# Order of projections, openings and turns, and products of constants in TensorE's waits, in a transformer forward pass of three mixers

## The reference

```python
def conv_ffn(h, w_up, conv_w, conv_b, w_down):
    u = causal_conv3_per_channel(h @ w_up) + conv_b
    gate, val = jnp.split(u, 2, axis=-1)
    return (jax.nn.silu(gate) * val) @ w_down      # 1024 -> 2 x 2816 -> 1024

# mixer 1: 12 heads of 64, causal softmax attention with a learned decay, q and k normed by head
# mixer 2: latent queries (256) and keys/values (128), 12 heads of 96 (64 plain, 32 rotary), causal
# mixer 3: 8 query heads and 2 key heads of 64, window of 128, partial rotary, a sink logit per head,
#          beside a gated depthwise convolution of 31 taps with layer norm and silu
# each mixer also attends to a memory of 256 tokens (4 heads of 64), and all parts go through w_out
```

## Time and profile before

| what | value |
|---|---|
| median of 3 runs | 2228.28 us (2227.41 to 2228.83) |
| profiled execution | 2224.88 us |
| its span | 2223.1 us, 30649 instructions |
| TensorE products busy | 2117.9 us (95%), 11378 |
| TensorE weight loads busy | 1759.9 us (79%) |
| VectorE busy | 1274.8 us (57%), 2212 |
| ScalarE busy | 952.9 us (43%), 1912 |
| GpSimd busy | 33.7 us (2%) |
| mean granted TensorE clock | 0.982 |
| HBM | 187.36 MB moved, 84 GB/s |

### The profile page before, as it was taken

How to read it: one execution, slowest core, us unless ns; L and a number is a source line. 1 busy time by engine, 2 the same in 40 slices (tenths; PEclk the granted TensorE clock), 3 DMA queues, 4 the chain that set the end, 5 groups by cost and what they waited for, 6 DMA issues and landing times.

```text
span 2223.1 us, 30649 instructions
## 1 busy us (share of the span) xinstructions
PE 2117.9 (95%) x11378; PEld 1759.9 (79%) x11378; DVE 1274.8 (57%) x2212; ACT 952.9 (43%) x1912; POOL 33.7 (2%) x71
## 2 busy tenths in 40 slices
PE   6999998999999798989999999999998889999999
PEld 6888786888889676768888888888888667888887
DVE  6645567746764775567367544434447865543442
ACT  6645544423445764444244343223344564332331
POOL 0000001000000010000000000000001000000000
PEclk9999999999999899989999999999999999999999
DMA  6212132332333010222333233333232112333332
GB/s 203 73 53 58 49 91 62 102 103 90 95 100 105 15 39 29 71 76 95 100 94 100 95 95 100 95 97 98 90 100 62 39 30 81 105 99 91 103 96 91
DMA packets 101670, 187.36 MB, mean 84 GB/s; under 512 B 11408, under 2 KB 12048, under 8 KB 101264
## 3 DMA queue, kind: packets, MB, share of 16 engines
q1 hardware_dynamic: 101520, 185.39, 27.5%
HBM read 183.25 MB, written 2.10 MB: 83 GB/s over the span
## 4 chain that ended last, share of the span: by engine, by line
PE 47%; DVE 3%; ACT 2%; issue 1%; POOL 0%; DVEq 0%; ACTq 0%; POOLq 0%
PE PSA L1541 15%; PE PSA L1542 14%; PE PSA L1543 14%; PE PSA L1559 1%; PE PSA L1560 1%; PE PSA L1561 1%; DVE RS L1694 1%; DVE WL L1705 0%; ACT PP L2043 0%; ACT WH L1974 0%; PE PSA L1648 0%; PE PSA L1663 0%; DVE CV L1694 0%; PE PSA L1630 0%; DVE XT L1846 0%
## 5 line engine op out<-in xcount | busy, mean ns | idle before, releaser
L1705 DVE TENSOR_TENSOR WL<-RAW,WH 128x512 fp32r<-128x512 f32 x681 | 459.2, 690 | 470.7 <-ACT WH L1974 447.1
L1974 ACT ACTIVATE WH<-RAW 128x512 fp32r<-128x512 f32 x681 | 414.7, 626 | 485.5 <-PE PSA L1543 407.1
L1541 PE MATMUL PSA<-HNh,WH 128*128 128x512 f32 x1440 | 566.3, 393 | 28.5 <-DVE CV L1694 21.2
L1542 PE MATMUL PSA<-HNl,WH 128*128 128x512 f32 x1440 | 562.9, 391 | 0.0
L1543 PE MATMUL PSA<-HNh,WL 128*128 128x512 f32 x1440 | 562.8, 391 | 0.0
L1541 PEld LDWEIGHTS PSA<-HNh,WH 128*128 128x128 f32 x1440 | 272.0, 189 | 89.6 <-DVE CV L1694 22.0
L1542 PEld LDWEIGHTS PSA<-HNl,WH 128*128 128x128 f32 x1440 | 272.0, 189 | 57.3 <-issue 1.2
L1543 PEld LDWEIGHTS PSA<-HNh,WL 128*128 128x128 f32 x1440 | 271.8, 189 | 56.9
L1541 PE MATMUL PSA<-Gh,WH 128*128 128x512 f32 x704 | 274.3, 390 | 0.9 <-DVE Gl L1869 0.9
L1542 PE MATMUL PSA<-Gl,WH 128*128 128x512 f32 x704 | 273.9, 389 | 0.0
L1543 PE MATMUL PSA<-Gh,WL 128*128 128x512 f32 x704 | 273.9, 389 | 0.0
(11 more groups left out here) (253 smaller groups left out, 2478.1 us busy)
## 6 DMA issues: line engine op xcount, KB each, us to landing
RAW<-in_w SPq DMA_DIRECT2D x681, 256.0 KB, 2.6
XT<-in_x SPq DMA_DIRECT2D x8, 256.0 KB, 5.3
MT<-in_mem SPq DMA_DIRECT2D x2, 1024.0 KB, 6.4
out_x<-XT SPq DMA_DIRECT2D x8, 256.0 KB, 2.1
PAR<-in_par SPq DMA_DIRECT2D x1, 207.0 KB, 7.2
CB<-in_cb SPq DMA_DIRECT2D x1, 100.0 KB, 7.1
PAR<-in_par SPq DMA_DIRECT2D x1, 84.5 KB, 2.0
CONST<-in_const SPq DMA_DIRECT2D x1, 65.0 KB, 5.3
```

What stands on the lines that cost most here:

```text
L1541: pe.matmul(out, wh, xh, start=(a["start"] and c == 0), stop=False)
L1542: pe.matmul(out, wh, xl, start=False, stop=False)
L1705: dve.tensor_tensor(l[:, :], r[:, :], h[:, :], ALU.subtract).then_inc(done.sem("split.dve"), 1)
L1974: act.activation(h[:, :], r[:, :], ACT.Copy).then_inc(done.sem("split.act"), 1)
```

## The change

1. `out_parts` opens chunks 0, 2, 4 and 6 and closes them in the order of the chunks, each closed one followed by the whole one behind it. Squares and additions are written 5 and 6.2 beats after each chunk instead of behind all of them; `Norm` keeps the order of the additions in `adds`.
2. `ffn` loses `ahead`: one pair is opened before `total`, in all four calls, and every later group is scaled before the next is opened.
3. V of the second mixer is copied by VectorE (`vevac`) 0.5 beats after ScalarE's copy of the keys, and this frees the bank.
4. Third mixer: the turn of the keys is written 3 beats later, those of the queries 2.5; for its pairs (`both`) `pbcast` and what follows (`sums`) come behind the transposes instead of ahead of the values; `psink` is written with the last maximum.
5. `WARM`: ahead of thirteen steps, TensorE multiplies an identity by a constant of 384 columns 3 to 22 times, 117 times in all, into a bank that the planner sees as free for four beats. Nobody reads the result. If no bank is free nothing is written.

```diff
 def out_parts(first, late):
-    return ([(c, first, late) for c in range(OPEN)] + [(c, late, 8) for c in range(OPEN)]
-            + [(c, first, 8) for c in range(OPEN, 8)])
+    return ([(2 * c, first, late) for c in range(OPEN)]
+            + [x for c in range(OPEN) for x in ((2 * c, late, 8), (2 * c + 1, first, 8))])
...
+WARM = {("totalc", "mem0"): 12, ("qturn", (0, 1)): 12, ("pbcast", (0, 1)): 8, ("pscore", (0, 2, 0)): 12,
+        ("pscore", (1, 0, 1)): 5, ("pturn", (1, 0, 0, 0)): 22, ("pturn", (1, 0, 1, 0)): 6, ("pscore", (1, 6, 1)): 8,
+        ("pscore", (2, 0, 0)): 10, ("pscore", (2, 1, 3)): 3, ("spreadout", 0): 9, ("pturn", (2, 4, 3, 0)): 4,
+        ("pvals", (2, 5, 0)): 6}
...
         def step(kind, key, **a):
+            if (kind, key) in WARM:
+                warm((kind, key), WARM[kind, key])
...
+        def warm(key, n):
+            banks = [b for b in pick(8, range(8)) if ready(psum.freed[b], 4)]
+            if banks:
+                psum.take(("warm", key), [], banks[0])
+                step("warm", key, n=n, bank=banks[0])
...
+                elif k == "warm":
+                    w.wait_ge(s_cb, 16)
+                    for t in psum.before["warm", key]:
+                        w.wait_ge(*done(*t))
+                    for _ in range(a["n"]):
+                        pe.matmul(PS[a["bank"]][:, 0:384], IDB, CB[:, 0:384], start=True, stop=True)
...
+                    if i == 3 and job.sink is not None:
+                        step("psink", jkey, job=job, S=S, last=key + (0 if t.joint else 1,))
...
+            def older(self, scored, turned):
+                ends = turned and turned[1] == 3
+                late = ends and self.jobs[turned[0]].both
+                cost = self.sums(*turned) if ends and not late else 0
+                cost += self.values(*turned) if turned else 0
+                cost += self.turn(*scored) if scored else 0
+                return cost + (self.sums(*turned) if late else 0)
...
             def fed(d, c):
                 added(name, layer, c, first, d)
-                norm.got.append(("project.dve", (name, layer, c, first)))
+                norm.got[c] = ("project.dve", (name, layer, c, first))
                 norm.part(c, norm.free, 1.3)
+                after(5, lambda: norm.square(c))
+                after(6.2, lambda: norm.add(c))
...
-            for c in range(KC):
-                after(0.5 + 1.3 * c, lambda c=c: norm.square(c))
-                after(1.7 + 1.3 * c, lambda c=c: norm.add(c))
...
-                    if (s, q) == (0, 0):
-                        opened = [both(n) for n in range(ahead)]
-                    groups = opened[q] if q < len(opened) else both(q)
-                    for x, (g, b) in enumerate(groups):
+                    first = (s, q) == (0, 0)
+                    opened = [up_group(x) for x in range(2)] if first else []
+                    for x in range(2):
+                        g, b = opened[x] if first else up_group(x)
                         last.scaled(g, b)
...
+                if late:
+                    after(0.5, lambda: step("vevac", (g, t), copy=late(dst, t, PS[bank][:, 0:width])))
...
-                psum.take(("up", g, t), [("evac.act", (g, t))], bank)
+                psum.take(("up", g, t), [("vevac.dve" if late else "evac.act", (g, t))], bank)
...
-                      [([yt[:, t, :] for t in range(4)], BK[0][:, :], BK[1][:, :], par("gk2"), lambda: [])])
+                      [([yt[:, t, :] for t in range(4)], BK[0][:, :], BK[1][:, :], par("gk2"), lambda: [])], lags=(2, 2, 3.5, 7, 2.5))
...
-                 for x in range(2)], h, QR[:, 3 + p, :], 2.0)
+                 for x in range(2)], h, QR[:, 3 + p, :], 4.5)
```

More of the change, by code:

```diff
@@ L618, in part @@
                 step("part", (self.name, c), norm=self, c=c, got=self.got[c], free=free, h=h)
[L619 removed]
+                self.out[c] = (h, l, [("part.dve", (self.name, c))])
                 def low():
@@ L636, in add, with all_fed @@
             def add(self, c):
-                step("feed", (self.name, c), norm=self, c=c, sq=("feed", self.name, c))
+                step("feed", (self.name, c), norm=self, c=c, sq=("feed", self.name, c), last=self.adds[-1:])
+                self.adds.append(c)
+            def all_fed(self):
+                return [self.fed(c) for c in range(KC)]
             def feed(self, c, got):
-                self.got.append(got)
+                self.got[c] = got
                 if self.free is not None:
@@ L646, in finish @@
             def finish(self, free):
-                if not self.out:
+                if None in self.out:
                     for c in range(KC):
@@ L791, in values, with sums, spread @@
                     psum.take(("pvals", jkey), [("pmix.mul", ckey)], 6)
[L792 to L801, removed]
-                step("pvals", key, job=job, i=i, jkey=jkey, t=t)
-                return 0.3 * job.tiles[i][1] / 128 + (0.8 if i == 3 else 0)
+                step("pvals", key, job=job, i=i, jkey=jkey, t=t)
+                return 0.3 * job.tiles[i][1] / 128
+            def sums(self, n, i):
+                jkey, ckey = (self.id, n), (self.id, self.jobs[n].chunk)
+                need([("precip.dve", jkey)])
+                aux = aux_bank(("pbcast", jkey), [("pspread.act", ckey)])
+                step("pbcast", jkey, S=PSTAT[pstats.of[jkey]], bank=aux)
+                def spread():
+                    x = tmp.take(("pmix", ckey), [("pmix.dve", ckey)])
+                    step("pspread", ckey, jkey=jkey, bank=aux, F=TMP[x], before=tmp.before["pmix", ckey])
+                    after(0.4, lambda: self.mix(n))
+                after(0.3, spread)
+                return 0.8
             def recip(self, n):
@@ L807, in recip @@
                 S = PSTAT[pstats.of[jkey]]
-                if job.sink is not None:
-                    step("psink", jkey, job=job, S=S, last=(self.id, n, 3, 0 if self.at[self.id, n, 3].joint else 1))
                 step("precip", jkey, job=job, S=S, last=(self.id, n, 3))
@@ L876, in projection, with ffn @@
             until([("part.dve", (norm.name, KC - 1))], 0)
-            for c in range(KC):
-                after(0.5 + 1.3 * c, lambda c=c: norm.square(c))
-                after(1.7 + 1.3 * c, lambda c=c: norm.add(c))
-        def ffn(f, gate, up, down, layer, off, last, conv, weight, norm, between=None, ahead=1):
+        def ffn(f, gate, up, down, layer, off, last, conv, weight, norm, between=None):
             ring[:], aux_ring[:] = [0, 1, 2, 3, 4], [5, 6]
@@ L884, in ffn @@
             for s in range(2):
-                parts, opened = [], []
-                def both(q):
-                    c, key = HALF * s + q, (f, s, q)
-                    freed = [[("conv.dve", (key, x))] for x in range(2)] if conv else [[("silu.act", key)], [("gated.mul", key)]]
-                    return [dense(n, layer, col, last.out, t)
-                            for (n, col), t in zip(((gate, 128 * c), (up, off + 128 * c)), freed)]
+                parts = []
                 for q in range(HALF):
@@ L957, in wide, with up @@
             return g
-        def up(name, p, parts, copies, take, each):
+        def up(name, p, parts, copies, take, each, late=None):
             g, n0, cols = dense_at[0], tiles_at[0], up_cols(name, p)
@@ L1718, in vector @@
                     w.wait_ge(*done("square.act", key))
-                    if c == 0:
+                    if not a["last"]:
                         dve.tensor_copy(nm.acc, S[:, 0:nm.N]).then_inc(done.sem("feed.dve"), 1)
                     else:
-                        w.wait_ge(*done("feed.dve", (nm.name, c - 1)))
+                        w.wait_ge(*done(*nm.fed(a["last"][0])))
                         dve.tensor_tensor(nm.acc, nm.acc, S[:, 0:nm.N], ALU.add).then_inc(done.sem("feed.dve"), 1)
```

43 lines of the change are left out of this document (26 added, 17 removed).

## The result

The changed kernel takes **2216.99 us**, median of 4 runs (2213.43 to 2218.14), against 2228.56 for the kernel before in the same session: ratio 0.9949, 95% interval 0.9933 to 0.9965. That is 11.6 us faster where 44 were forecast, outside the range. The profiled execution took 2213.43 us, its span is 2211.6, and its granted clock 0.990 against 0.982 before. It was the fastest of the four: the others took 2216.53 to 2218.14 us, at a granted clock of 0.985 or 0.986.

The account below looks back on a forecast made before the run. TensorE sets the end, so gains are its idle or half-clock time: 29.2 + 12.5 + 3.5 + 1.5 - 2 = 44.7 us off the profiled 2224.88 gives 2180.2, as a median 2184 us; range 2168 to 2205.

Parts of the forecast that it names:

- Openings: Feed-forward openings: earlier sum of squares and new closing order save 10.9 us in layer 0, 16.2 in layer 1, 2.1 in the last.
- half of the 6.2 as won: Layer 1's opening: of 6.2 us beyond layer 0's work, evenly spaced closing wins 3.1 despite about five additions.
- The bound named: Layer 1's opening: additions ahead of the last low half could cost up to 3.5 us.
- the last addition ends before group 2 does: Feed-forward openings: with squares that early, the earlier sum is not waited for.
- Constants: All three mixers: 117 products in waits hold TensorE's clock, 12.5 us won, 2 us lost where they outlast the wait.
- Rival C: Fewer of the thirteen groups of constants happen, or part of the wait was elsewhere: 6 us less, 2190; chance 0.1.
- Later turns and sums: Third mixer: waits on GpSimd's rotation shrink, 3.5 us; sums behind the transposes save 1.5 us.
- V by VectorE: Second mixer: VectorE copying V frees ScalarE but holds a bank longer; 0, between 3 us won and 5 lost.
- B: Openings' wait moves to the third and fourth pair, 3 to 4 us each, in two layers: 2199; chance 0.13.
- A: Products of constants don't hold the clock or outlast their waits: none of the 12.5, 3 more lost, 2199; chance 0.15.
- E: Slower: scaling each group before opening the next starves TensorE once per pair; at 1 us a pair 2272; chance 0.03.
- What was to show it: Signs for and against, such as sum some 11 us after a layer's first product, or later last low halves.

Follow-up runs that it names:

- e5: The changed kernel with squares and additions behind all eight chunks again, the new order of closing kept; 2203.59 us, ratio 0.9895.
- e4: The changed kernel with the old projection (`out_parts`): chunks 0 to 3 closed in a row, squares and additions late; 2199.64 us, ratio 0.9880.
- e6: The changed kernel with chunks 0 to 3 closed in a row as before, but squares and additions early; 2209.53 us, ratio 0.9920.
- e1: The kernel before with the new `ffn` (opening of the feed-forward layers) alone; 2208.14 us, ratio 0.9916.
- e11: e4 with its late squares and additions 0.9 beats apart instead of 1.3; 2196.74 us, ratio 0.9870.
- e12: e4 with the old lags of the third mixer's turns, the sums as changed; 2205.37 us, ratio 0.9906.
- e7: e4 with V copied by ScalarE again; 2199.03 us, ratio 0.9874.

## Why the prediction was wrong

Of the 44.7 us forecast, 33 did not come. By step:

**Openings, 29.2 forecast, 7.9 measured (3.5, 9.5 and -5.1).** This is the step that failed. The half on the earlier sum was right: the 10.59 us waits went, no new ones took their place in the third and fourth pair, and scaling each group first shows no cost there. The one wait on a split in layer 0's opening is 0.9 us, at 361.87. What failed is the sentence on layer 1 that set "about five additions of some 0.7 us" ahead of "the last low half" against the even spacing and took "half of the 6.2 as won", and its silence for the other layers: "The 1.27 us wait for the last chunk's low half stays". The additions came in all three projections, and with them the squares on ScalarE, which the prediction never put ahead of ScalarE's weight splits. Together they are 1.04 us a chunk (0.51 for the additions, 0.42 for the squares, 0.11 not placed), and from H to S 9 to 13 us in three layers. The even spacing, taken as 3.1 us won in layer 1, is worth 2.5 there with late squares (e5 against e4); with early ones it loses 1.1 (20.8 against e6's 19.7). The bound named, "3.5", was for one layer and one engine.

A second error is smaller and shows in e1, where the openings alone win 20.0 us of stage time. That "the last addition ends before group 2 does" holds only with early squares: with late ones, in e1, the product of sums waits 2.37, 1.12 and 2.35 us. The two facts pull against each other: early squares free the sum and delay the halves, late ones the reverse. e11 has most of both, 24.2 us of the 29.2.

**Constants, 12.5 less 2 forecast; 1.6 measured in the changed kernel, 4.2 to 6.9 in three others.** The mechanism holds, the size was two to three times too large. With a granted clock of 1.00 the first mixer's stretch is 2.8 us shorter where 4.0 were forecast, and 1.7 is the mean of five pairs. That waits for ScalarE and VectorE take back what TensorE gains is likely, but not shown. Rival C's condition was met: four of thirteen places have no products. Why the changed kernel shows less than the others is open; the difference is within the intervals.

**Later turns and sums, 3.5 and 1.5 forecast, 4.5 to 6 and 0.5 to 2 measured.** Right in mechanism, a little low in size (and the two parts of the first term add up to 3.7, not 3.5): the waits on GpSimd went whole, where the lags were to take only part, and in e12 half clock stands behind a wait on GpSimd as well, which the prediction left out.

**V by VectorE, 0 forecast, some 3 us lost** by the profiles, inside the bounds given (3 won to 5 lost). The row compared was a copy's duration; what counted was what stands ahead of it in VectorE's queue.

**Second mixer.** It lost 4.2 us: 3 is V, and the rest is less than kernels with the same second mixer differ by (286.6 to 291.7 us).

**Rivals.** B had the right actors, "the squares and the late low halves", but put their wait into the third and fourth pair; they came before the sum. Its 2199 was still 18 us too low, as it kept half of the openings and all of the constants. A, B and C were priced one at a time, and parts of all three happened at once. E stayed away: no starving per pair.

**What was to show it.** Sum some 11 us after the first product: 19.6. No wait over 2 us in the openings: 2.89 and 2.63, and twice 2.9 in the last layer. Clock 1.00 in the first mixer: yes. Mostly 1.00 behind the second mixer's first scores: 0.83 in 720 to 740, 0.75 before. 117 products: 93. Waits on GpSimd below 1.5: gone. And the first sign of "wrong" that the prediction listed for the openings was the one that came: "the last low half of a projection later than before", 11.7 us against 6.1.

## What to carry to other kernels

Before moving a small step earlier, write out the loop that runs at that place through every engine's queue (here high half, split, low half, addition), and add the moved step to each queue it enters; an engine at 42% busy had no room in just that loop. Then price the same stretch once for every layer that has it. A wait that is removed by two moves together deserves a test of each alone: here the opening alone gave 19 us and the whole change 12.

## What the runs showed of the hardware

A copy of V, 128 partitions by 256 from PSUM, took 477 ns on VectorE (twelve in e4) and 477 ns on ScalarE (twelve in e7): no engine is quicker at it. The Trainium skill (VectorE: DVE Perf Modes, The TRN2 errata) gives, as estimates, 392 and 357 ns; the measurement decides. TensorE's granted clock fell to 0.50 (1.2 GHz) some 2 us after a single wait of 2.89 us had ended, in the changed kernel (0.98 in 314 to 316, 0.50 in 316 to 319), and stood at 0.50 right behind one of 2.81 us in e12. Behind 22 products of constants it was 1.00 in 731.5 to 735, a stretch that holds most of the wait of 2.21 us, and behind that wait 0.63 in 735 to 738. A product of 384 bf16 columns was 323 ns long at least, 326 in the median.
